# A two-block network on one core: latents' norms tile by tile, state space pairs in three streams, and four steps of the second block moved

## The reference, cut to what matters

```
first block:  hn = rmsnorm(x);  proj = hn @ w_in          # u 1024, c_q 512, c_kv 256, k_pe 64
  y_ssm = S5(u): complex scan s_t = a * s_(t-1) + Bbar u_t per group, y = Re(C s) + D u, gelu, GLU
  q  = rmsnorm(c_q)  @ w_uq;   kv = rmsnorm(c_kv) @ w_ukv    # 8 heads, rope on 64 of 192
  y_mla = causal softmax(q k^T) v
  h = x + concat(rmsnorm(y_ssm), rmsnorm(y_mla)) @ w_out;  h += conv_ffn(rmsnorm(h))
second block: u = rmsnorm(rmsnorm(h));  P = u @ w_in_2       # z, xbc, dt, and RWKV's r, k, v, ...
  dt = softplus(dt_raw + bias);  y_ssd = chunked SSD(xbc, dt) * silu(z), rmsnorm in 4 groups
  y_rwkv = wkv7(r, w, k, v, a, b) per head, groupnorm, bonus, gate
  h += concat(y_ssd, y_rwkv) @ w_out_2;  h += swiglu(rmsnorm(h));  rmsnorm
```

## Time and profile before

| | |
|---|---|
| median of three runs | 3042.41 us |
| the profiled execution, own time | 3044.3 us |
| its span | 3042.5 us |
| granted TensorE clock, mean | 0.980 |
| DVE, ACT, GpSimd busy | 69%, 51%, 22% |
| HBM | 155 GB/s over the span |

### The profile page before, as it was taken

How to read it: one execution, slowest core, us unless ns; L and a number is a source line. 1 busy time by engine, 2 the same in 40 slices (tenths; PEclk the granted TensorE clock), 3 DMA queues, 4 the chain that set the end, 5 groups by cost and what they waited for, 6 DMA issues and landing times.

```text
span 3042.5 us, 52413 instructions
## 1 busy us (share of the span) xinstructions
PE 2904.1 (95%) x21006; PEld 2597.6 (85%) x21006; DVE 2109.5 (69%) x3455; ACT 1565.9 (51%) x2611; POOL 679.6 (22%) x869
## 2 busy tenths in 40 slices
PE   7877999999999999899899999998999999999998
PEld 7766998888888889888788888997888888888887
DVE  7778877775777656677777776777656665566654
ACT  6445555553555545456555565455445444444443
POOL 0456301210112100565555550001000110011100
PEclk9888999999999999999999999999999999999999
DMA  6311455555555556332222223454555555655554
GB/s 254 115 56 58 165 180 187 188 177 191 201 192 194 166 171 224 112 108 95 77 91 97 99 91 105 146 182 155 175 170 187 185 192 173 203 193 194 185 172 142
DMA packets 79826, 475.34 MB, mean 156 GB/s; under 512 B 8225, under 2 KB 11297, under 8 KB 38305
## 3 DMA queue, kind: packets, MB, share of 16 engines
q1 hardware_dynamic: 76768, 459.66, 43.7%
q10 hardware_dynamic: 2816, 12.32, 1.2%
HBM read 465.66 MB, written 6.29 MB: 155 GB/s over the span
## 4 chain that ended last, share of the span: by engine, by line
PE 77%; DVE 10%; issue 6%; ACT 4%; POOL 2%; DMA 0%; SPq 0%; ACTq 0%; POOLq 0%; DVEq 0%
PE bank L716 33%; PE bank L720 22%; PE bank L718 6%; PE bank L719 5%; DVE m L1233 2%; PE bank L738 1%; ACT m L2150 1%; POOL m L2860 1%; PE bank L1029 1%; POOL m L2856 1%; PE bank L1033 1%; PE bank L1140 0%; PE bank L991 0%; PE bank L998 0%; PE bank L915 0%
## 5 line engine op out<-in xcount | busy, mean ns | idle before, releaser
L720 PE MATMUL bank<-m,m 128*128 128x256 f32 x6864 | 1930.6, 281 | 0.0
L716 PE MATMUL bank<-m,m 128*128 128x512 f32 x4736 | 1657.2, 394 | 5.7 <-DVE m L2025 5.7
L1233 DVE TENSOR_TENSOR m<-m,m 128x1024 fp32r<-128x1024 f32 (+1 forms) x944 | 1072.2, 1144 | 614.2 <-ACT m L2150 607.4
L720 PEld LDWEIGHTS bank<-m,m 128*128 128x128 f32 x6864 | 1300.4, 189 | 0.9
L2150 ACT ACTIVATE m<-m 128x1024 fp32r<-128x1024 f32 (+1 forms) x944 | 911.8, 979 | 716.9 <-PE bank L720 692.8
L716 PEld LDWEIGHTS bank<-m,m 128*128 128x128 f32 x4736 | 890.9, 188 | 203.8 <-DVE m L2025 5.9
L718 PE MATMUL bank<-m,m 128*128 128x256 f32 x2128 | 637.5, 300 | 35.7 <-DVE m L1233 23.3
L719 PE MATMUL bank<-m,m 128*128 128x256 f32 x2128 | 605.1, 284 | 0.0
L718 PEld LDWEIGHTS bank<-m,m 128*128 128x128 f32 x2128 | 410.3, 193 | 59.6 <-issue 38.8
L719 PEld LDWEIGHTS bank<-m,m 128*128 128x128 f32 x2128 | 410.7, 193 | 1.9
L2836 POOL TENSOR_TENSOR m<-m,m 128x256 fp32r<-128x256 f32 x44 | 63.5, 1442 | 682.9 <-ACT m L2412 682.9
(11 more groups left out here) (382 smaller groups left out, 2893.0 us busy)
## 6 DMA issues: line engine op xcount, KB each, us to landing
m<-in_w_up SPq DMA_DIRECT2D x88, 1024.0 KB, 4.8
m<-in_w_down SPq DMA_DIRECT2D x128, 704.0 KB, 4.0
m<-in_w_gu SPq DMA_DIRECT2D x88, 1024.0 KB, 4.8
m<-in_w_out SPq DMA_DIRECT2D x48, 1024.0 KB, 5.1
m<-in_w_krv SPq DMA_DIRECT2D x48, 1024.0 KB, 4.8
m<-in_w_xbc SPq DMA_DIRECT2D x24, 1024.0 KB, 4.7
m<-in_w_z SPq DMA_DIRECT2D x16, 1024.0 KB, 4.8
m<-in_w_in SPq DMA_DIRECT2D x14, 1024.0 KB, 5.3
```

The lines of the kernel that those rows point to most:

```text
L716: pe.matmul(bank.rearrange("p (a b) -> p a b", a=2), hi, x, start=kc == L.k0, stop=False)
L720: m = pe.matmul(ps, lo, x[:, 0, :], start=False, stop=last)
L1233: v.tensor_tensor(lo_of(k), raw_of(k)[0], hi_of(k).bitcast(F32), SUB).then_inc(*lo_v(("lo", k)))
```

## The change

What it does, in the order of the diff:

- `sparse` makes each step of a generator last two. It is put around the sine tables of the later pairs and around `steps_dt`.
- `after(1)` begins four steps later (step 48 for 44); the others stay.
- State space pairs run in three streams instead of two, still one every three steps, and each has one step more: DVE's products and the scans are now two steps apart, GpSimd's sums a step later, PE's exit six steps behind its entry instead of five. `output` comes a step later.
- Heads: two streams of two heads each, three steps apart (`heads_of`), 26 steps for 24.
- `L_in2` waits for tiles 4 and 5 instead of 4 to 7. The squares of its tiles are taken one tile behind, and summed on PE two tiles behind. N_q's rate is formed while `L_kpe` runs, its outputs when `L_kpe` has used the first half of the activations (they are written over those). N_kv's rate, its outputs, the rotation of k_pe and its masks stand between tiles of `L_uq`. The banks of `L_uq` and `L_uk` change places.
- `angles` move from the start of `L_in2` to the setup's steps 18 to 21, the DMA of the positions with them.
- `norm_ssd`: one empty step more before the sums on PE, before the rate on DVE and before the norm on ACT. `halves_of_y` begins in step 30.

```diff
+def sparse(g):
+    for _ in g:
+        yield
+        yield
...
-    afters = timed(*((AFTER + ROUNDS * b, after(b)) for b in range(8)))
+    afters = timed(*((AFTER + ROUNDS * b + 4 * (b == 1), after(b)) for b in range(8)))
...
-    pairs = [timed(*((OPEN + 6 * c + 3 * p, pair(c, p)) for c in range(8))) for p in range(2)]
-    ahead = timed(*((OPEN + 6 * c + 1, tables(c + 1)) for c in range(7)))
-    outs = timed(*((OPEN + 6 * c + 9, output(c)) for c in range(8)))
+    pairs = [timed(*((OPEN + 3 * k, pair(k // 2, k % 2)) for k in range(n, 16, 3))) for n in range(3)]
+    ahead = timed(*((OPEN + 6 * c + 1, sparse(tables(c + 1))) for c in range(7)))
+    outs = timed(*((OPEN + 6 * c + 10, output(c)) for c in range(8)))
...
+def heads_of(head):
+    streams = [timed(*((6 * j + 3 * p, side(head(4 * j + 2 * p), head(4 * j + 2 * p + 1))) for j in range(4)))
+               for p in range(2)]
+    return side(*streams)
+
+def side(*gens):
+    live = list(gens)
+    while live:
+        for g in list(live):
+            try:
+                next(g)
+            except StopIteration:
+                live.remove(g)
+        if live:
+            yield
...
# tensor: pair(c, p), between entry and exit
-                for _ in range(5):
+                for _ in range(6):
                     yield
# tensor: mla
+            def latents():
+                def add(t):
+                    if t in (8, 12):
+                        pe.wait_ge(*ev_v["in", 6 + (t == 12)])
+                    add_square(*latent(t))
+                def turn_q(t):
+                    if t == 1:
+                        rope(0, kpe, ev_v["kpe"], norm_v["ms", N_q.id])
+                    elif t > 8:
+                        rope(t - 8, qp[:, t - 9, :], ev_a["q", t - 1])
+                adds = Lag(L_in2, lambda t: None, lambda t: None, add)
+                yield from linear(L_in2, nrhs, lambda kc: cut_of(N_attn, kc), done=adds,
+                                  free=[[ev_v["in", 4]], [ev_v["in", 5]]])
+                yield from linear(L_kpe, nrhs, lambda kc: cut_of(N_attn, kc), ev_v["in", 12])
+                adds.tail()
+                yield
+                yield from linear(L_uq, lambda kc: cqr[:, :, kc, :], lambda kc: cut_of(N_q, kc), done=turn_q,
+                                  free=[[ev_v["in", 13]], [ev_v["kpe"]]])
             def mla():
-                add_squares(N_q)
-                add_squares(N_kv)
-                yield
-                pe.wait_ge(*norm_v["ms", N_q.id])
-                rope(0, kpe, ev_v["kpe"])
-                yield
-                yield from linear(L_uq, ...)
+                yield from latents()
...
# tensor: norm_ssd
                 yield
+                yield
                 add_squares(N_ssd[g])
...
# vector: mla
-                v.wait_ge(*lin_pe["tile", L_kpe.number(0)])
-                norm(N_q)
-                norm(N_kv)
-                yield
-                rope(0, kpe)
-                ...
-                yield from linear(L_uq, lambda t: rope(t - 8, qp[:, t - 9, :]) if t > 8 else None)
+                yield from linear(L_in2, first(L_in2))
+                norm_rate(N_q)
+                yield from linear(L_kpe, lambda t: None)
+                v.wait_ge(*lin_pe["piece", L_kpe.place[0, 7][0]])
+                norm_outs(N_q)
+                scaled(kpe, 0, L_kpe, 0, N_attn, "kpe")
+                yield
+                def turn_q(t):
+                    if t == 0:
+                        norm_rate(N_kv)
+                    elif t == 2:
+                        rope(0, kpe)
+                        ...
+                    elif t == 3:
+                        norm_outs(N_kv)
+                    elif t > 8:
+                        rope(t - 8, qp[:, t - 9, :])
+                yield from linear(L_uq, turn_q)
...
-            second_mixer(main(), block, tail, after, timed((STEPS, steps_dt())), both_rates(ffn_v.last),
+            second_mixer(main(), block, tail, after, timed((STEPS, sparse(steps_dt()))), both_rates(ffn_v.last),
...
-                       timed((31, halves_of_y())))
+                       timed((30, halves_of_y())))
...
# scalar: mla
-                a.wait_ge(*lin_pe["tile", L_kpe.number(0)])
-                for i in range(4):
-                    square(N_q, i, ev_v["in", 8 + i])
-                norm(N_q)
-                for i in range(2):
-                    square(N_kv, i, ev_v["in", 12 + i])
-                norm(N_kv)
+                squares_ = Lag(L_in2, lambda t: None, squared)
+                yield from linear(L_in2, squares_)
+                squares_.tail()
+                yield from linear(L_kpe, lambda t: norm_rr(N_q))
+                norm_highs(N_q)
+                yield
+                yield from linear(L_uq, evacuate)   # norm_rr(N_kv) at tile 1, norm_highs(N_kv) at tile 3
```

More of the change, by code:

```diff
@@ L645, in program, with latent @@
         N_last = Norm(norms, hchunks, ("norm_f_g_2", 0), hchunks, D, 1e-6, 7)
+        def latent(t):
+            return (N_q, t - 8) if t < 12 else (N_kv, t - 12)
         def cut_of(N, i):
@@ L1170, in tensor_program @@
             setup = timed((1, first_squares()), (8, s5_transposed()), (11, s5_k0()))
[L1171 to L1175, removed]
+            first_mixer(chain(linear(L_in, nrhs, lambda kc: cut_of(N_attn, kc)), paired(mla()),
+                              heads_of(head), paired(mla_out())), setup, s5_pair,
                         lambda c: iter(range(3)), lambda c: iter(range(1)))
@@ L1584, in angles @@
                 v.wait_ge(*mla_v.last)
-                run(sincos(mla_v, pos, ak, ar_, csn, ash, mla_a, "rope"))
+                yield from sincos(mla_v, pos, ak, ar_, csn, ash, mla_a, "rope")
                 yield
@@ L2063, in setup @@
                 yield from s5_tables(0)
+                yield
+                yield
+                yield from angles()
             v.wait_ge(ld_vec, 16)
@@ L2073, in vector_program @@
             v.wait_ge(ld_cst, 16)
-            before = chain(angles(), linear(L_in2, first(L_in2)),
-                           linear(L_kpe, lambda t: scaled(kpe, 0, L_kpe, 0, N_attn, "kpe")), mla())
-            first_mixer(chain(first_layer(), paired(before), flight(head, 16, 4), paired(mla_out())), setup(),
+            first_mixer(chain(first_layer(), paired(mla()), heads_of(head), paired(mla_out())), setup(),
                         s5_pair, s5_tables, s5_output)
@@ L2655, in scalar_program @@
             setup = timed((0, first_squares()), (5, rate(N_attn)), (7, s5_ab()), (9, s5_transposed()), (10, s5_cz()),
-                          (11, s5_ca()), (15, s5_tables(0)))
-            before = chain(angles(), linear(L_in2, lambda t: None), linear(L_kpe, lambda t: None), mla())
-            first_mixer(chain(linear(L_in, lambda t: None), paired(before), flight(head, 16, 4), paired(mla_out())),
-                        setup, lambda c, p: iter(range(6)), s5_tables, s5_output)
+                          (11, s5_ca()), (15, s5_tables(0)),
+                          (18, angles()))
+            first_mixer(chain(linear(L_in, lambda t: None), paired(mla()), heads_of(head), paired(mla_out())),
+                        setup, lambda c, p: iter(range(7)), s5_tables, s5_output)
             a.wait_ge(*s5_a["y", 7])
@@ L2785, in mla @@
             def mla():
-                g.wait_ge(*lin_pe["tile", L_kpe.number(0)])
+                yield from linear(L_in2)
+                yield from linear(L_kpe)
                 norm(N_q)
-                norm(N_kv)
                 yield
-                yield
-                yield from linear(L_uq)
+                yield from linear(L_uq, lambda t: norm(N_kv) if t == 3 else None)
                 yield from linear(L_uk)
@@ L2898, in pool_program @@
                 g.memset(q, 0.0).then_inc(*s5_g(*([("zero", 1)] if q is Cz1[1] else [])))
-            before = chain(iter(range(1)), linear(L_in2), linear(L_kpe), mla())
-            first_mixer(chain(linear(L_in), paired(before), flight(head, 16, 4), paired(mla_out())),
+            first_mixer(chain(linear(L_in), paired(mla()), heads_of(head), paired(mla_out())),
                         timed((15, s5_tables(0))), s5_pair, s5_tables, lambda c: iter(range(1)))
```

45 lines of the change are left out of this document (28 added, 17 removed).

## The result

The changed kernel takes 3025.28 us in the median of five runs (3020.68 to 3033.38), against 3042.3 for the kernel before beside it (3041.41 to 3042.52): a ratio of 0.9949, 95% interval 0.9939 to 0.996. That is 17 us faster where 39 were forecast, and 1 us outside the range. The profiled execution was the slowest of the five (3033.38, span 3031.6), so its stretches are compared with those of before, not its end.

The account below looks back on a forecast made before the run. TensorE, busy 2904.1 of 3042.5 us, was taken as the bound overall, with a chain of waits from latents to heads. Terms 5 + 17 + 0 + 3 + 5 + 5 + 4.5 = 39.5 off 3042.4 gave 3003 us, range 2984 to 3024.

Parts of the forecast that it names:

- part c: Heads in two staggered streams, 26 steps instead of 24: 0 us, bounds 12 faster to 21 slower.
- The loop: In the heads, a cycle of waits through POOL, DVE and ACT, 11.5 us, said to close every other period.
- rival 1: The heads give it back: each period takes 11.5 us, 21 more in all; 3024 us, chance 0.12.
- short order: In the heads, periods without ACT's copy-out behind the diagonals, where DVE and PE alone make about 7.5 us.
- a: Start of L_in2: PE no longer waits for the evacuation of tile 7; -5.0 us, bounds 3.0 to 6.5.
- b: Latents' norms made tile by tile, so the heads start earlier; -17 us, bounds 8 to 28.
- e: Softplus in RWKV's rounds spread over 28 steps instead of 14; -5 us, between 1 and 9.
- f: Norm sums of the groups a step later, ending PE's waits for their squares; -5 us, bounds 2 to 6.5.
- g: Halves of y a step earlier, ending PE's wait at L_outr; -4.5 us, bounds 1 to 5.7.
- d: Second preparation four steps later, shortening DVE's wait for POOL's first solve; -3 us, bounds -6 to +2.
- upper bound of c: Heads 12 us faster; doubted because GpSimd shares its SBUF interface with DVE.
- Rival 2: The clock stays low from the end of tile 13 to the last head; 19.5 slower, 3062 us, chance 0.04.

Follow-up runs that it names:

- e11: The changed kernel with only the state space output (DVE's sum and ACT's gelu) one step later; 3021.47 us, ratio 0.9936.
- e3: The changed kernel with only GpSimd's squares of the heads one step later in its queue; 3010.75 us, ratio 0.9897.
- e5: The changed kernel with pairs in two streams, tables in consecutive steps and heads in one flight, all as before; 3006.72 us, ratio 0.9883.
- e2: The kernel before with only the heads changed, to two staggered streams; 3046.38 us, ratio 1.0015.
- e8: The changed kernel with only the pair's first two sums on GpSimd one step earlier, ahead of the heads' squares; 3032.95 us, ratio 0.9968.
- e6: e3 with the second preparation back at its old step and the groups' norm sums back one step; 3022.09 us.
- e10: e5 with the second preparation back at its old step; 3010.78 us.
- e7: e3 with softplus in 14 consecutive steps again and the halves of y a step later, as before; 3025.93 us.
- e9: e5 with the heads in two staggered streams and GpSimd's squares a step later; 3009.01 us, ratio 0.9891.

## Why the prediction failed, step by step

**The failing step** is in part c: "It closes only where ACT's queue has the copy-out behind the diagonals, which is every other period; in the others DVE and PE alone make about 7.5." The loop and its price were right for the periods that it was followed through, 11.5 us forecast against 11.3 and 11.9 measured. The mean was wrong because I had followed one way round the loop and took the period without it for free. In that period the copy-out stands behind the gelu, which waits for a DVE sum, which waits behind the next pair's products. e11 moved this output alone and these periods fell from 11.5 to 9.4: even then not to 7.5. So c was 0 in the sum and 19.4 in the profile (95.8 for 76.4); it is rival 1, which had 12% and gave 3024. Against it the prediction set "half of the periods have the short order". That was read from the order of instructions on ACT; what it lacked was the same walk through the second kind of period. The order of POOL's queue accounts for 12 to 14 of the 19.4 us (e3); the 6 that e3's heads still have above 76.4 are not divided by any run.

The forecast without c can be tested by e5: 3006.7, where the sum gives 3003, for c was 0 in it. Part of that nearness is luck: in e5's own profile a is 6.0, b 11.4, e 5.3, f 5.8 to the end of the span and g 3.7, and d -0.5, some 32 of the 37 us between the two profiles and not 39.5; the rest is 3.2 in the heads (73.2 for 76.4) and 2.4 in the rest of the first block, which I had not counted.

| term | forecast | measured | from |
|---|---|---|---|
| a start of L_in2 | -5.0 | -5.0 to -6.3 | stretch 0 to 384, all twelve profiles that hold the edit, against 63.9 before (62.8 in e2, also without it) |
| b latents' norms | -17 | -10.8; -7.1 (e8) to -15.6 (e3) over all twelve | start of L_kpe (matmul 672) to the first scores, 85.3 before (83.0 in e2) |
| c pairs and heads | 0 | +19.4 | heads, 95.8 for 76.4; in time 19 to 22 (e5 against the changed kernel) |
| d second preparation | -3 | 0 to -1 | e6, e10 |
| e softplus | -5 | -2 to -7 | e7's row against those with the edit, -2.3 and -3.4 against the changed kernel and e3; the round itself 84.4 to 79.1 |
| f groups' norm sums | -5 | -5.8 to -6.7 | e6, to the end of the span and to the last matmul |
| g halves of y | -4.5 | -1.5 to -2.7 | e7; the wait of 5.7 fell to 0.6 |

Part b: the wait before L_uq is 5.8 us where I had 3 to 5, the clock was 0.83 and not above 0.9, and the heads began at 183.8 and not at 177. DVE reached 78% of the 61.8 us behind that wait, where I took 85%. The size was off by 6, within the bounds of 8 and 28; in the slowest profiles, e8 and e9, it is 7.1 and 7.6, below them.

Part d: DVE's wait at the first solve fell only from 10.2 to 7.0, and not under 4:

```profile
DVE m L1862 <- POOL m L2933: 7.0, 1, 7.0
```

The prediction had the solve end at the same place "whatever the queues do". Counted from matmul 6212 it begins at the same place (66.6 and 66.5) and ends at 118.1 us for 115.1: the solve itself takes 3 us longer while the second preparation stands later, 51.5 for 48.6. In e6 and e10, which put that preparation back, it ends at 115.0 again. What lengthens it was not traced. The new wait at the second solve came as forecast, 2.9 us. PE's 6.1 behind the cut went and its 6.1 at the second setup fell to 2.6, but one of 6.6 at line 1035, in the rounds' blocks, came in their place. I had counted what the request gains and 3 us given back at the second solve, but not that the first solve takes longer.

Part e: the round with softplus shortened by 5.3, as forecast, but the rounds behind gave 1 back in the changed kernel (the row fell by 4.2). Part g: the wait lost 5.1 us, and the stretch 2.5 in the changed kernel and 3.7 in e3 and e5. In both parts the named cost went as said, and not all of it was time; what stood next on the path was not traced.

DVE's work in the heads, 63 to 65 us in the kernels before, changed and e5, is the lower bound that e5's 73.2 comes nearest to. The Trainium skill (GPSIMD Engine Reference, 1. Specifications) speaks of contention of GpSimd with DVE instructions that have two SBUF inputs. The product that I had cited for it fell from 977 ns to 684 in the changed kernel, while the scans beside it rose from 454 to 628: so the dearer instructions are others now, and DVE's sum over the heads stayed within 2 us. No run isolates GpSimd's share in either figure. The forecast's doubt that the upper bound of c can be had was neither borne out nor refuted. Rival 2, a clock low all through, did not come: the granted clock is 0.75 in the heads of the changed kernel and 0.84 in those of e5. PE is idle for the same share of both, 32%, so the idle share alone doesn't explain the difference.

## What to carry to other kernels

In a cyclic schedule over in-order queues, write down for each kind of period what stands directly ahead of every operation of the suspected loop, on every engine, and assume that the loop closes in all kinds until each has been walked through; a period that looks open on one engine may be closed by another engine's queue. Before a step is added to a stream, look at which other stream's waiting instruction it lands behind: one yield on GpSimd was worth 12 to 14 us of the heads here, and another, placed by the same idea without that look (e8), brought the loss back by a new door. Several edits that need each other on paper should be timed in groups: the five small ones and the latents' norms were worth 36 us by themselves, and the streams took 20 of it back.

## What the hardware showed that I had not expected

The time of one and the same program on one core spreads along with the granted clock. The ten runs of the changed kernel go from 3020.68 us at a mean clock of 0.985 to 3033.38 at 0.980, 13 us for 0.005; between them stand, among others, 3023.3 at 0.983, 3025.28 at 0.984, 3025.52 at 0.982, 3028.53 at 0.981 and 3031.45 at 0.981. A straight line through all ten gives 2.4 us for each 0.001, with single runs some us off it. The kernel before spreads by 10 us (3037.37 to 3047.25 over all sets). The profiles show one place of it: from the latents to the heads PE runs in bursts with pauses, and which burst falls on the low clock differs between executions of the same code. In the two profiles of the changed kernel the 48 matmuls from the 768th take 13.6 us at a granted clock of 0.87 and 15.2 at 0.77. Between matmuls 672 and 912, e3 and e6, which are the same code there, take 154.6 and 160.8 us; why their difference is larger than that of one program's two profiles (173.2 and 171.0) is not shown. A gain of 3 us in a kernel with such a stretch is to be read from its own stretch of the trace, not from the median, and if it lies in that stretch, from several profiles.

ACT's table loads take 1.28 us each (the row at 222.82 above, and one more for the exponents behind it), two in each pair of periods. The first of them stands in the loop's way and costs nothing all the same: it ends at 224.10, and the gelu's operand comes 0.28 us later.
